# The tail of a mixture-of-experts kernel: TensorE forms the weighted sum of two expert rows, four gather buffers

## The chip, the cores and the metric

The kernel runs on one core of a Trainium2 chip. The metric is the time of one execution on the device in microseconds, as the median of the runs. A profiled execution has a time of its own, and its span runs from the first to the last instruction.

## The reference, cut to what matters

The program is a two-part transformer. What the change touches is the very end: the last mixture-of-experts layer, the residual, and the final norm. `second_block` ends so (`h` has 1024 tokens of 1024 features behind 16 meta tokens, which are cut off):

```
v = rms_norm_2(h, norm2_g[l])
h = h + hier_moe(v, ...)           # each token: 2 of 16 experts, weighted
return rms_norm_2(h[:, N_META:], final_g)

# in hier_moe
y = y + comb[:, e:e + 1] * (he @ exp_w2[e])     # comb: two weights per token, else 0
```

So for each token: h + w0 * (row of its first expert) + w1 * (row of its second expert), then an RMS norm over the features with a gain.

## The kernel before

`moe_phase` (line 2598) is the last of the phases. Tokens are sorted by expert into slots; 31 tiles of 128 slots (`NTILE`) are computed one after another. For each tile j, POOL fetches 128 normed token rows with an indirect DMA (`slots_in`, 2715) into one of two halves of `xs`, TensorE transposes them (`slots_t`, 3037), multiplies them with the expert's weights (`up`, 3045; `down`, 3057), ACT copies the result from PSUM (`YP`) to `yt` (2808), and POOL stores it to the DRAM tensor `expert_out` (2722). The weights pass through `stage`, five slots of 1024 columns: SP loads them, ACT rounds them to `whi`, DVE makes the rest `wlo` (`split_w`, 2837).

When all tiles are stored comes the tail, which is what the change rewrites. It goes over 8 token tiles (`NTT`) of 128 tokens, each 128 partitions by 1024 features in `ht`:

- POOL (2736 to 2747) waits for the last stores, and then for each token tile t issues two indirect DMAs of 512 KB, one for each of the token's two experts, into `yg[:, t % 3]`. There are three such buffers, so from t = 3 on it waits until tile t - 3 is added (`comb_done`).
- DVE (`combine`, 2975) waits for the two gathers, and adds w0 times the first and w1 times the second to `ht` by two instructions (2977, 2978). `cw` holds the weights, one for each partition and tile. The order on DVE is: combine(0), and then for each t: combine(t + 1), wait for the reciprocal root of tile t, multiply tile t by it and by the final gain (2987).
- ACT (2825 to 2831) waits for `comb_done` of tile t, squares it into `stage[:, 0]` with a running sum (2827), and turns the sum into the reciprocal root by Ln (2829) and Exp (2831). Each of the two needs its own load of a function table.
- SP (2708 to 2710) stores each finished tile to `y`.

TensorE has nothing to do in the tail. All engines work in the order in which their instructions are written; what passes between them are semaphores. `yg` lies in the space of the residual `E.X` that the tail no longer needs (columns 2 D to 8 D); `xs` lies behind it (8 D to 10 D). `TX` and `YP` are two PSUM tensors of 128x1024 f32.

Products on operands of the type `F32R` (experts, `whi`, `uhi`) and on plain `F32` both occur in the kernel. Plain f32 products with 512 columns are in the lines 1108 (sum of squares with a matrix of ones), 1130 and 3001 (router logits, two halves of 8 calls: 16 calls).

Of the kernel before, what the change touches and what calls it, by code (L numbers as in the profile page):

```python
# [19 lines left out]
ALU = mybir.AluOpType  # L20
# [3 lines left out]
P = 128  # L24
D = 1024
# [17 lines left out]
NTT = T // P  # L43
NSPARE = 15
NTILE = NE + NSPARE
# [90 lines left out]
def offsets(widths):  # L136
    at, n = {}, 0
    for name, w in widths:
        at[name] = (n, w)
        n += w  # L140
    return at, n


CONST_AT, CONST_N = offsets(CONST_WIDTHS)
# [4 lines left out]
def col(tile, at, name, j=None, w=1):  # L149
    o, width = at[name]  # L150
    if j is None:
        return tile[:, o:o + width]
    return tile[:, o + j:o + j + w]
# [14 lines left out]
def phase(nc, ctx):  # L168

    mine = []

    def sb(name, shape, dt=F32):
        return ctx.enter_context(nc.sbuf_tensor(f"{name}_{nc_tag(nc)}", shape, dt))

    def ps(name, shape, dt=F32):
        return ctx.enter_context(nc.psum_tensor(f"{name}_{nc_tag(nc)}", shape, dt))

    def sem(name):  # L180


        if not name.startswith("gp_"):
            mine.append(ctx.enter_context(nc.semaphore(f"{name}_{nc_tag(nc)}")))
            return mine[-1]
        return nc.alloc_semaphore(f"{name}_{nc_tag(nc)}")

    used = sorted(s.num for s in TAGS["used"])
    while used:
        n = 1  # L190
        while n < len(used) and used[n] == used[0] + n:
            n += 1
        nc.gpsimd.sem_clear(range(used[0], used[0] + n))
        used = used[n:]
    TAGS["used"] = mine
    return sb, ps, sem
# [5 lines left out]
def load_exp_ln(nc):  # L202

    nc.scalar.preload_act_table_set("natural_log_exp_and_others")
# [2393 lines left out]
def moe_phase(nc, E, dram):  # L2598


    with ExitStack() as ctx:
        sb, ps, sem = phase(nc, ctx)
        NS, R = 5, 8
        flat = E.X[:].rearrange("p k n -> p (k n)")
# [1 line left out]
        rows_of = [sb(f"token_rows{i}", [P, D])[:] for i in range(1)]  # L2606
        xs = flat[:, 8 * D:10 * D].rearrange("p (t n) -> p t n", n=D)
        yt = flat[:, 0:2 * D].rearrange("p (t n) -> p t n", n=D)
        yg = flat[:, 2 * D:8 * D].rearrange("p (t r n) -> p t r n", r=2, n=D)
        ht = sb("h_tokens", [P, NTT, D])  # L2610
        fgain = sb("final_rows", [P, D])
        rows_of += [fgain[:]]
        stage = sb("expert_stage", [P, NS, D])
# [20 lines left out]
        cw = sb("comb_w", [P, 2, NTT])  # L2634
# [3 lines left out]
        idx = sb("slot_index", [P, 2 * NTT], mybir.dt.uint32)  # L2638
        tcmp = flat[0:1, 2 * D + 2560:2 * D + 2560 + NSPARE * NE].rearrange("p (s e) -> p s e", e=NE)
        tsum, texp = sb("spare_count", [1, NSPARE]), sb("spare_expert", [1, NSPARE], mybir.dt.int32)  # L2640
        TX, YP = ps("slots_t", [P, D]), ps("expert_out", [P, D])
# [4 lines left out]
        wr_in, small_in, wr_ready, t_done, copied, squared, ms_ready, rs_ready, half_done, half_copied, logits_done = (  # L2646
            sem(n) for n in ("router_loaded", "small_loaded", "router_ready", "transposed", "copied", "squared",
                             "mean_square_ready", "rstd_ready", "logits_t_done", "logits_t_copied", "logits_done"))
# [5 lines left out]
        w_hi, w_lo, used = sem("expert_hi_ready"), sem("expert_lo_ready"), sem("expert_used")  # L2654
        u_hi, u_lo, h_t, silu_done, h_ready, h_hi, h_lo, y_ready = (sem(n) for n in (
            "slots_hi_ready", "slots_lo_ready", "hidden_t_done", "silu_done", "hidden_ready", "hidden_hi_ready",
            "hidden_lo_ready", "expert_out_ready"))
        idx_ready, fgain_in = sem("index_ready"), sem("final_gain_loaded")
        xs_in, y_out = [sem(f"gp_slots_loaded{i}") for i in range(2)], [sem(f"gp_expert_stored{i}") for i in range(2)]
        y_in = [sem(f"gp_expert_gathered{i}") for i in range(3)]  # L2660
        comb_done, f_sq, f_ms, f_rs, out_ready, steps = (sem(n) for n in (
            "combined", "final_squared", "final_mean", "final_rstd_ready", "out_ready", "dve_steps"))
        load_exp_ln(nc)
        block = ctx.enter_context(nc.Block())

        units, first_up, first_down = [], {}, {}
        for j in range(NTILE + 1):
# [6 lines left out]
        NU = len(units)  # L2674
        ahead = {}
        for j in range(NTILE + 1):
            end = first_up[j + 1] if j + 1 < NTILE else first_down[NTILE - 1] if j + 1 == NTILE else NU
            start = first_up[j] if j < NTILE else first_down[NTILE - 1]
# [34 lines left out]
        @block.gpsimd  # L2713
        def _(eng):
            def slots_in(j):
                if j >= 2:
                    eng.wait_ge(t_done, NTT + j - 1)
                eng.indirect_dma_start(
                    out=xs[:, j % 2, :], out_offset=None, in_=dram["normed"][:, :],
                    in_offset=bass.IndirectOffsetOnAxis(ap=inv[:, j:j + 1], axis=0)).then_inc(xs_in[j % 2], 16)  # L2720

            def expert_out(j):
                eng.wait_ge(y_ready, j + 1)
                eng.dma_start(dram["expert_out"][P * j:P * j + P, :], yt[:, j % 2, :]).then_inc(y_out[j % 2], 16)

            for s in range(NU_ROWS):
                eng.wait_ge(u_stored[s], 16 * ((NTT - s + NU_ROWS - 1) // NU_ROWS))
            eng.wait_ge(inverse_ready, 1)
            slots_in(0)
            slots_in(1)  # L2730
            for j in range(NTILE + 2):
                if j + 2 < NTILE:
                    slots_in(j + 2)
                if j >= 2:
                    expert_out(j - 2)
            for b in range(2):
                eng.wait_ge(y_out[b], 16 * ((NTILE - b + 1) // 2))
            eng.wait_ge(idx_ready, 1)
            for t in range(NTT):
                if t >= 3:  # L2740
                    eng.wait_ge(comb_done, t - 2)
                for r in range(2):
                    eng.indirect_dma_start(
                        out=yg[:, t % 3, r, :], out_offset=None, in_=dram["expert_out"][:, :],
                        in_offset=bass.IndirectOffsetOnAxis(ap=idx[:, NTT * r + t:NTT * r + t + 1], axis=0)).then_inc(y_in[t % 3], 16)
            for b in range(3):
                eng.wait_ge(y_in[b], 32 * ((NTT - b + 2) // 3))

        @block.scalar
        def _(eng):  # L2750
# [83 lines left out]
        def _(eng):  # L2834
            chain = Chain(eng, steps)
# [122 lines left out]
            for j in range(NTILE + 1):  # L2958
# [13 lines left out]
                for n in ahead[j][4:]:  # L2972
                    split_w(n)

            def combine(t):
                eng.wait_ge(y_in[t % 3], 32 * (t // 3 + 1))
                chain(eng.scalar_tensor_tensor(ht[:, t, :], yg[:, t % 3, 0, :], cw[:, 0, t:t + 1], ht[:, t, :], ALU.mult, ALU.add))
                eng.scalar_tensor_tensor(ht[:, t, :], yg[:, t % 3, 1, :], cw[:, 1, t:t + 1], ht[:, t, :],
                                         ALU.mult, ALU.add).then_inc(comb_done, 1)

            combine(0)
# [8 lines left out]
        def _(eng):  # L2990
            ident, ones = (col(E.con, CONST_AT, n) for n in ("ident", "ones"))
# [36 lines left out]
            for s in range(NTT):  # L3028
                mm = eng.matmul(POS[:, NE * s:NE * NTT], before_b[:] if s == 0 else ones_b[:], rows[:, 0:NE * (NTT - s)],
                                start=s == 0, stop=s == NTT - 1, skip_group_check=True)  # L3030
            mm.then_inc(pos_done, 1)
            eng.wait_ge(places_ready, 3)
            for i in range(2 * NTT):
                mm = eng.matmul(INV[:, 0:2 * NTILE], col_hot[:, i, :], tok_at[:, i, :], start=i == 0, stop=i == 2 * NTT - 1)
# [22 lines left out]
            def down(j, c):  # L3057
                n = first_down[j] + c
                eng.wait_ge(w_lo, n + 1)
                uh, ul = (u[:, j % 2, P * c:P * c + P] for u in (hhi, hlo))  # L3060
                for lhs, w, first, last in ((uh, whi, c == 0, False), (uh, wlo, False, False), (ul, whi, False, c == 1)):
                    for q in range(2):
                        mm = eng.matmul(YP[:, 512 * q:512 * q + 512], lhs, w[:, n % R, 512 * q:512 * q + 512],  # L3063
                                        start=first, stop=last)
                mm.then_inc(used, 1)

            slots_t(0)
            for j in range(NTILE + 1):
                if j < NTILE:
                    eng.wait_ge(u_lo, j + 1)  # L3070
                    if j >= 2:
                        eng.wait_ge(h_ready, j - 1)
                    for i in range(3):
                        up(j, i)
                if j >= 1:
                    eng.wait_ge(h_ready, j)
                    if j >= 2:
                        eng.wait_ge(h_lo, j - 1)
                    for c in range(2):
                        mm = eng.transpose(HT[:, P * c:P * c + P], hid[:, (j - 1) % 2, P * c:P * c + P], ident)  # L3080
                    mm.then_inc(h_t, 1)
                if j < NTILE:
                    up(j, 3)
                if j + 1 < NTILE:
                    slots_t(j + 1)
                if j >= 1:
                    eng.wait_ge(h_lo, j)
                    if j >= 2:
                        eng.wait_ge(y_ready, j - 1)
                    for c in range(2):  # L3090
                        down(j - 1, c)

# [295 lines left out]
```

## Time and profile before

| | us |
|---|---|
| median of 3 runs | 3211.17 |
| lowest, highest | 3204.91, 3211.19 |
| profiled execution | 3202.6 |
| its span | 3200.8 |
| tail: first gather issued to the end of the span | 3153.7 to 3200.8 |
| TensorE busy, whole span | 2804.8 (88%) |
| DVE, ACT busy, whole span | 1668.0 (52%), 1297.0 (41%) |

Times of rows are counted from the start of the span. TensorE is the busiest engine over the whole span, but it is idle in the tail, so the shares of the whole say nothing about the stage that is changed; that stage is read from its own rows. A record of a matmul has a modelled end: the distance between the starts of two that follow each other is the better measure of what one costs. The granted clock is given as a share of 2.4 GHz.

### The profile page before, as it was taken

The numbers are of one execution on the slowest core, as the hardware profiler recorded it, in microseconds if no ns is written. First come the engines' busy times: TensorE is split into PE (matmuls) and PEld (weight loads), VectorE is DVE, ScalarE is ACT, GpSimd is POOL, SyncE is SP. The second block draws the span as 40 slices with busy tenths as digits, with TensorE's granted clock in tenths as the row PEclk, the third lists the DMA queues.
The fourth block names the chain that finished last, engine by engine and source line by source line (L and its number), as shares of the span: only waits on it lengthen the run. The fifth ranks groups of instructions, "written<-read, shape, count | busy, mean of one in ns | idle before, by whom it ended". The sixth has DMA issues, their size and how long they took to land. (4 is left out here: it accounts for less than half of the span.)

```text
span 3200.8 us, 36024 instructions
## 1 busy us (share of the span) xinstructions
PE 2804.8 (88%) x13684; PEld 2195.9 (69%) x13684; DVE 1668.0 (52%) x2723; ACT 1297.0 (41%) x2204; POOL 196.3 (6%) x283
## 2 busy tenths in 40 slices
PE   7999998987887999995986999999989899588883
PEld 3777885656776868883654799987856588376672
DVE  5566545657774340013773356641134482688885
ACT  4444212446775141123442231111324411487886
POOL 0000000110000000000000000000000030011112
PEclk8999998989998999996998999999989999799997
DMA  5233444533303042222124123322353251599996
GB/s 230 97 132 119 171 148 122 153 100 97 80 20 120 7 152 76 89 79 87 33 83 157 61 83 103 129 96 79 112 169 80 58 180 33 198 346 346 366 357 236
DMA packets 143999, 431.05 MB, mean 135 GB/s; under 512 B 19874, under 2 KB 44194, under 8 KB 142548
## 3 DMA queue, kind: packets, MB, share of 16 engines
q1 hardware_dynamic: 99572, 264.52, 24.7%
q0 software_dynamic: 26512, 93.80, 8.5%
q10 hardware_dynamic: 17744, 70.43, 6.0%
q8 instruction: 109, 1.79, 0.2%
q14 instruction: 62, 0.51, 0.1%
HBM read 322.21 MB, written 106.47 MB: 134 GB/s over the span
## 5 line engine op out<-in xcount | busy, mean ns | idle before, releaser
L1099 PE MATMUL acc<-act_hi,w_hi 128*128 128x512 f32 (+3 forms) x2512 | 721.5, 376 | 62.4 <-DVE act_lo L856 41.5
L1099 PE MATMUL acc<-act_lo,w_hi 128*128 128x512 f32 (+3 forms) x2512 | 701.0, 368 | 0.0
L1099 PE MATMUL acc<-act_hi,w_lo 128*128 128x512 f32 (+3 forms) x2512 | 699.3, 367 | 0.0
L1099 PEld LDWEIGHTS acc<-act_hi,w_hi 128*128 128x128 f32 x2512 | 449.1, 189 | 165.3 <-DVE w_lo L761 57.6
L761 DVE TENSOR_TENSOR w_lo<-w_stage,w_hi 128x1024 fp32r<-128x1024 f32 x126 | 154.3, 1225 | 737.7 <-ACT w_hi L582 737.7
L1099 PEld LDWEIGHTS acc<-act_lo,w_hi 128*128 128x128 f32 x2512 | 447.0, 190 | 75.8
L1099 PEld LDWEIGHTS acc<-act_hi,w_lo 128*128 128x128 f32 x2512 | 446.1, 189 | 76.4
L582 ACT ACTIVATE w_hi<-w_stage 128x1024 fp32r<-128x1024 f32 x126 | 133.1, 1057 | 846.8 <-PE acc L1099 819.7
L2843 DVE SCALAR_TENSOR_TENSOR expert_lo<-expert_stage,params,expert_hi 128x512 fp32r<-128x512 f32 x248 | 172.5, 747 | 64.2 <-ACT expert_hi L2759 64.0
L1949 DVE TENSOR_REDUCE max<-scores 128x1 f32<-128x256 f32 (+6 forms) x256 | 117.4, 484 | 149.2 <-PE scores L2092 148.3
L2759 ACT ACTIVATE expert_hi<-expert_stage,params 128x512 fp32r<-128x512 f32 x248 | 163.2, 713 | 64.3 <-DMA expert_stage<-in_exp_w 30.4
L2132 PE MATMUL outputs<-probs_t,v_ones 128*128 128x512 f32 (+2 forms) x392 | 172.1, 520 | 1.9 <-ACT probs_t L1893 1.9
L1893 ACT ACTIVATE probs_t<-scores_t 128x512 f32<-128x512 f32 (+4 forms) x196 | 100.2, 513 | 119.9 <-PE scores_t L2118 116.9
L2110 PE MATMUL scores_t<-q_stack,k_hi 128*128 128x512 f32 (+4 forms) x196 | 122.6, 625 | 2.5 <-ACT q_rows L1917 2.5
L1480 DVE TENSOR_REDUCE stats<-scores 128x1 f32<-128x1280 f32 (+1 forms) x72 | 100.7, 1398 | 44.0 <-PE scores L1592 44.0
L3052 PE MATMUL expert_up<-expert_hi,slots_hi 128*128 128x512 f32 x248 | 101.7, 410 | 7.1 <-DVE slots_lo L2851 7.1
L693 ACT ACTIVATE out_stage<-acc 128x512 f32<-128x512 f32 (+1 forms) x162 | 78.0, 544 | 64.7 <-PE acc L1099 64.7
L1407 ACT ACTIVATE probs<-scores,stats 128x1280 f32<-128x1280 f32 (+1 forms) x80 | 92.1, 1153 | 25.8 <-DVE stats L1481 24.7
L2088 PE MATMUL scores<-k_hi,q_stack 128*128 128x256 f32 (+6 forms) x256 | 95.0, 374 | 5.5 <-DVE max L1949 2.6
L3054 PE MATMUL expert_up<-expert_hi,slots_lo 128*128 128x512 f32 x248 | 98.5, 397 | 0.0
L3053 PE MATMUL expert_up<-expert_lo,slots_hi 128*128 128x512 f32 x248 | 98.2, 396 | 0.0
L2092 PE MATMUL scores<-k_lo,q_rows 128*128 128x256 f32 (+6 forms) x256 | 92.2, 367 | 0.0
(409 smaller groups left out, 4210.8 us busy)
## 6 DMA issues: line engine op xcount, KB each, us to landing
expert_stage<-in_exp_w SPq DMA_DIRECT2D x186, 512.0 KB, 6.3
w_stage<-in_w_in SPq DMA_DIRECT2D x43, 512.0 KB, 4.2
rope<-out_stage ACTq DMA_DIRECT2D x26, 640.0 KB, 3.6
proj<-out_stage ACTq DMA_DIRECT2D x26, 640.0 KB, 5.0
slots_out<-residual POOLq DMA_DIRECT2D x31, 512.0 KB, 6.7
w_stage<-in_ab_w_in SPq DMA_DIRECT2D x26, 512.0 KB, 4.7
w_stage<-in_gla_w_in SPq DMA_DIRECT2D x25, 512.0 KB, 4.7
residual<-in_adaln_w POOLq DMA_DIRECT2D x24, 512.0 KB, 3.8
```

The source lines that it names most:

```text
L582: eng.activation(whi[:, w % 2, :], stage[:, w % NSTG, :], ACT.Copy).then_inc(w_hi, 1)
L761: eng.tensor_tensor(wlo[:, w % 2, :], stage[:, w % NSTG, :], whi[:, w % 2, :].bitcast(F32), ALU.subtract).then_inc(w_lo, 1)
L1099: mmi = eng.matmul(a[:, t, 0:n], lhs[:, j.w % 2, kb:kb + P], rhs[:, c0 + k, off:off + n], start=first, stop=last)
L1480: chain(eng.tensor_reduce(st[:, q % 4, 0, 0:u.rows], s, AX, ALU.max))
L1893: eng.activation(pT[0:w, q % 3, c0:512], ST[q % 2][0:w, c0:512], ACT.Exp, scale=SCALE).then_inc(exped, 1)
L1949: eng.tensor_reduce(mx[:, n % 2, h, pc:pc + 1], SP[p % 3][:, 0:k1 - k0], AX, ALU.max).then_inc(max_done, 1)
L2110: eng.matmul(s[:, c0:512], kh[:, c, tok:tok + P], qs[:, n % QS, c0:512], start=True, stop=False)
L2132: eng.matmul(O[n % 2][:, c0:512], v1[0:w, u.pair % VS, u.side, tok // P, :], pT[0:w, q % 3, c0:512], start=fox and b == 0, stop=b == len(u ...
L2759: ins = eng.activation(whi[:, n % R, c], stage[:, n % NS, c], ACT.Copy, scale=gain_of(2 * i + q))
L2843: ins = eng.scalar_tensor_tensor(wlo[:, n % R, c], stage[:, n % NS, c], gain_of(2 * i + q), whi[:, n % R, c].bitcast(F32), ALU.mult, ALU.s ...
L3052: eng.matmul(UP[j % 2][:], uh, wh, start=k == 0, stop=False)
L3054: mm = eng.matmul(UP[j % 2][:], ul, wh, start=False, stop=k == KD - 1)
```

## The change

Six of the eight token tiles (all but 0 and 4) are "mixed". For each of them DVE builds two diagonal matrices of 128x128, the identity times the token weights, in slots 1 and 2 of `stage`, behind its last weight split. TensorE then forms, for each half of 512 features, diag(w0) times the first gathered rows plus diag(w1) times the second, by two plain f32 products that accumulate in PSUM; the result goes alternately to `TX` and `YP`. DVE adds it to `ht` by one instruction in place of two. Tiles 0 and 4 keep the old two instructions. The gather buffers become four, the last of which lies where `xs` was; so POOL waits also for the last slot transposes.

```
-        yg = flat[:, 2 * D:8 * D].rearrange("p (t r n) -> p t r n", r=2, n=D)
+        NG = 4
+        yg = flat[:, 2 * D:10 * D].rearrange("p (t r n) -> p t r n", r=2, n=D)
...
+        mixed = [t for t in range(NTT) if t not in (0, 4)]
+        diag = stage[:, 1:3, :].rearrange("p a (b n) -> p (a b) n", n=P)
+        MIX = [TX, YP]
...
             eng.wait_ge(idx_ready, 1)
+            eng.wait_ge(t_done, NTT + NTILE)
             for t in range(NTT):
-                if t >= 3:
-                    eng.wait_ge(comb_done, t - 2)
+                if t >= NG:
+                    eng.wait_ge(comb_done, t - NG + 1)
...
+            eng.wait_ge(w_lo, NU)
+            for i, t in enumerate(mixed):
+                for r in range(2):
+                    eng.tensor_scalar(diag[:, 2 * i + r, :], col(E.con, CONST_AT, "ident"), cw[:, r, t:t + 1], None,
+                                      ALU.mult).then_inc(diag_ready, 1)
...
             def combine(t):
-                eng.wait_ge(y_in[t % 3], 32 * (t // 3 + 1))
+                if t in mixed:
+                    i = mixed.index(t)
+                    eng.wait_ge(mixed_ready, i + 1)
+                    eng.tensor_tensor(ht[:, t, :], MIX[i % 2][:], ht[:, t, :], ALU.add).then_inc(comb_done, 1)
+                    return
+                eng.wait_ge(y_in[t % NG], 32 * (t // NG + 1))
...
+            eng.wait_ge(diag_ready, 2 * len(mixed))
+            eng.wait_ge(y_ready, NTILE)
+            for i, t in enumerate(mixed):
+                eng.wait_ge(y_in[t % NG], 32 * (t // NG + 1))
+                if i >= 2:
+                    eng.wait_ge(comb_done, mixed[i - 2] + 1)
+                for q in range(2):
+                    for r in range(2):
+                        mm = eng.matmul(MIX[i % 2][:, 512 * q:512 * q + 512], diag[:, 2 * i + r, :],
+                                        yg[:, t % NG, r, 512 * q:512 * q + 512], start=r == 0, stop=r == 1)
+                mm.then_inc(mixed_ready, 1)
```

## Rows read from the trace of the kernel before

**Rows 1.** The chain that ended last, tail: start us, us, what.

```profile
3163.07 1.15 ACT expert_stage L2827 x2
3164.23 1.28 ACT L2829
...
3196.49 1.28 DVE h_tokens L2987
```

**Rows 2.** Groups by line, 3146.2 to 3201: busy us, mean ns, idle time before.

```profile
L2987 DVE SCALAR_TENSOR_TENSOR h_tokens<-h_tokens,final_rstd,final_rows 128x1024 f32<-128x1024 f32 x8 | 10.3, 1284 | 6.0 <-ACT final_rstd L2831 6.0
L2829 ACT ACT_TABLE_LOAD x8 | 10.3, 1283 | 0.1
L2827 ACT ACTIVATE expert_stage<-h_tokens 128x1024 f32<-128x1024 f32 x8 | 8.3, 1042 | 12.8 <-DVE h_tokens L2978 12.8
L2829 ACT ACTIVATE final_rstd<-final_sum_sq,eps 128x1 f32<-128x1 f32 x8 | 2.4, 295 | 0.1
L2831 ACT ACTIVATE final_rstd<-final_rstd 128x1 f32<-128x1 f32 x8 | 1.6, 203 | 0.1
L2827 ACT ACTIVATION_READ_ACCUMULATOR expert_stage<-h_tokens 128x1 f32 x8 | 1.5, 186 | 0.0
```

**Rows 3.** DVE and ACT in order of time: start us, us, instruction [idle before].

```profile
3160.43 1.28 DVE L2977 SCALAR_TENSOR_TENSOR h_tokens<-residual,comb_w,h_tokens 128x1024 f32<-128x1024 f32 x1 [14.30 <-DMA residual<-slots_out,slot_index]
3163.79 1.28 DVE L2977 SCALAR_TENSOR_TENSOR h_tokens<-residual,comb_w,h_tokens 128x1024 f32<-128x1024 f32 x1 [0.76 <-DMA residual<-slots_out,slot_index]
3167.24 1.04 ACT L2827 ACTIVATE expert_stage<-h_tokens 128x1024 f32<-128x1024 f32 x1
3171.53 1.28 DVE L2987 SCALAR_TENSOR_TENSOR h_tokens<-h_tokens,final_rstd,final_rows 128x1024 f32<-128x1024 f32 x1 [0.36 <-ACT final_rstd L2831]
...
3192.20 1.04 ACT L2827 ACTIVATE expert_stage<-h_tokens 128x1024 f32<-128x1024 f32 x1
```

**Rows 4.** Stretches: us, busy by engine (count), granted clock, DMA share, GB/s.

```profile
3149.20:3153.80 4.60, 0.00 (x0) 0.00 (x0) 0.00 (x0) 1.02 (x1) 0.62 (x2) 1.00 0.28 114
3154.00:3201.00 47.00, 0.00 (x0) 0.00 (x0) 30.30 (x24) 32.92 (x48) 15.84 (x16) 0.50 0.74 268
3161.30:3163.80 2.50, 0.00 (x0) 0.00 (x0) 1.71 (x3) 0.73 (x1) 0.50 (x1) 0.50 0.98 357
50.20:54.50 4.30, 4.30 (x6) 1.81 (x6) 0.84 (x2) 3.37 (x4) 0.00 (x0) 0.50 0.77 278
2797.98:2802.20 4.22, 4.22 (x10) 3.35 (x11) 0.00 (x0) 1.20 (x2) 0.00 (x0) 0.50 0.63 241
```

**Rows 5.** DVE's groups by line and shape in the expert phase.

```profile
L2851 DVE TENSOR_TENSOR slots_lo<-slots_t,slots_hi 128x1024 fp32r<-128x1024 f32 x31 | 37.7, 1217 | 2.5 <-ACT slots_hi L2766 2.5
L2923 DVE TENSOR_SCALAR slot_tmp<-expert_up 128x128 f32<-128x128 f32 x1 | 0.3, 292 | 0.0
```

**Rows 6.** POOL's gathers: the first with a wait, the slowest issue, landing times.

```profile
3163.30 0.94 POOL L2743 DMA_INDIRECT residual<-slots_out,slot_index  x1 [2.36 <-DVE h_tokens L2978]
3167.91 1.56 POOL L2743 DMA_INDIRECT residual<-slots_out,slot_index  x1 [0.30 <-issue]
DMA to landing us min/median/max: 4.1/6.2/7.7
```

**Rows 7.** Plain f32 products of lines 3001 and 1130: ns min/median/max, first and last start.

```profile
L3001 PE MATMUL expert_up<-residual,router_w x32: 592/592/607, 2729.3 to 2750.4; 128*20 128x512 f32 x32
L1130 PE MATMUL branch_acc<-branch_work,consts x8: 590/592/596, 2223.2 to 2226.2; 128*128 128x512 f32 x8
```

**Rows 8.** TensorE in order of time, products of line 1108 at granted clock 0.50.

```profile
50.19 1.19 PE L1108 MATMUL acc<-square_sums,consts 128*128 128x512 f32 x1 [1.71 <-PEq L229]
52.03 1.91 PE L1108 MATMUL acc<-square_sums,consts 128*128 128x512 f32 x2
52.88 1.06 PE L1108 MATMUL acc<-square_sums,consts 128*128 128x512 f32 x1
```

**Rows 9.** One more stretch, columns as in rows 4.

```profile
1502.00:1512.00 10.00, 10.00 (x18) 5.12 (x19) 2.29 (x5) 3.78 (x3) 0.00 (x0) 0.50 0.15 59
```

More of the change, by code:

```diff
@@ L2659, in moe_phase @@
         xs_in, y_out = [sem(f"gp_slots_loaded{i}") for i in range(2)], [sem(f"gp_expert_stored{i}") for i in range(2)]
-        y_in = [sem(f"gp_expert_gathered{i}") for i in range(3)]
+        y_in = [sem(f"gp_expert_gathered{i}") for i in range(NG)]
+        diag_ready, mixed_ready = sem("weight_diagonals_ready"), sem("outputs_mixed")
         comb_done, f_sq, f_ms, f_rs, out_ready, steps = (sem(n) for n in (
@@ L2738, in _ @@
             eng.wait_ge(idx_ready, 1)
+            eng.wait_ge(t_done, NTT + NTILE)
             for t in range(NTT):
-                if t >= 3:
-                    eng.wait_ge(comb_done, t - 2)
+                if t >= NG:
+                    eng.wait_ge(comb_done, t - NG + 1)
                 for r in range(2):
                     eng.indirect_dma_start(
[L2744 to L2747, printed above, removed]
+                        out=yg[:, t % NG, r, :], out_offset=None, in_=dram["expert_out"][:, :],
+                        in_offset=bass.IndirectOffsetOnAxis(ap=idx[:, NTT * r + t:NTT * r + t + 1], axis=0)).then_inc(y_in[t % NG], 16)
+            for b in range(NG):
+                eng.wait_ge(y_in[b], 32 * ((NTT - b + NG - 1) // NG))
         @block.scalar
@@ L2973, in _ @@
                     split_w(n)
-            def combine(t):
-                eng.wait_ge(y_in[t % 3], 32 * (t // 3 + 1))
-                chain(eng.scalar_tensor_tensor(ht[:, t, :], yg[:, t % 3, 0, :], cw[:, 0, t:t + 1], ht[:, t, :], ALU.mult, ALU.add))
-                eng.scalar_tensor_tensor(ht[:, t, :], yg[:, t % 3, 1, :], cw[:, 1, t:t + 1], ht[:, t, :],
+            eng.wait_ge(w_lo, NU)
[3 more added lines that the diff above has]
+                                      ALU.mult).then_inc(diag_ready, 1)
+            def combine(t):
+                if t in mixed:
[4 more added lines that the diff above has]
+                eng.wait_ge(y_in[t % NG], 32 * (t // NG + 1))
+                chain(eng.scalar_tensor_tensor(ht[:, t, :], yg[:, t % NG, 0, :], cw[:, 0, t:t + 1], ht[:, t, :], ALU.mult, ALU.add))
+                eng.scalar_tensor_tensor(ht[:, t, :], yg[:, t % NG, 1, :], cw[:, 1, t:t + 1], ht[:, t, :],
                                          ALU.mult, ALU.add).then_inc(comb_done, 1)
```

## The prediction

> **What bounds the kernel now.** The change touches only the last 55 us, so I read the chain of waits there first: it shows which engine sets the end. After the last expert output is stored and the first gather has landed, the chain is ACT alone: square, table load, Ln, table load, Exp, again and again until the last DVE multiplication [rows 1]. The grouped lines of the same stretch give the pieces [rows 2]. For a token tile ACT has 1.042 (square) + 0.186 (accumulator read) + 1.283 + 0.295 + 1.283 + 0.203 = 4.29 us, which overlap a little at the joints; the table loads are 2.57 of it. The order of time says what a tile really costs: the second square starts at 3167.24 and the eighth at 3192.20, which is six steps of 4.16 us [rows 3]. ACT waits for DVE once, 12.8 us before the first square [rows 2]; behind that it has no gap. DVE has three instructions of 1.28 us a tile, 3.9 us, and a rest of 0.36 us in which it waits for ACT's rstd (the idle time of L2987) [rows 2, 3]. So DVE is nearly full and yet not the bound. TensorE does nothing from 3149.2 on; its granted clock is 1.00 until 3153.8 and 0.50 from 3154 to the end, the lower of its two levels (1.2 GHz) [rows 4].
>
> **The change, part by part.**
>
> *DVE's additions in six tiles.* Two instructions (1.280 + 1.285 us) become one tensor_tensor of 128x1024 with one operand in PSUM. The nearest row is L2851, same shape, PSUM and SBUF operands: 1.217 us [rows 5]. That frees 1.35 us of DVE a tile. On the path it is worth nothing while ACT needs 4.16 us a tile: DVE only waits longer for the rstd. Bound: if DVE did set the pace it would be 6 x 1.35 = 8.1 us (a rival below).
>
> *Twelve diagonal matrices.* Each is a tensor_scalar of 128x128. The nearest row is L2923, 0.292 us (with a PSUM operand); so at most some 12 x 0.3 = 3.6 us, and not below 0; I take the row [rows 5]. They stand behind the last hidden_lo, which ends at 3146.1, so they are through by 3149.8. DVE idles from there until 3160.43 (14.3 us) [rows 3]. Nothing else queues behind them before the gather: cost 0. Without that cover it would be 3.6.
>
> *The new waits.* POOL waits for the last slot transposes, long done when the last expert is computed: 0 to 0.1 us. TensorE waits for diagonals and the last expert output, done by 3150.3: 0.
>
> *Four gather buffers.* The two gathers of tile 3 go out right behind the first six, some 2 us earlier, not behind the addition of tile 0 (3163.30) [rows 6]. Nothing waited for that tile: after tile 1 DVE has no idle time on a gather. So the gain is 0. The cost is bounded by the load on the engines: between 3161.3 and 3163.8 both tile 3 and tiles 1 and 2 would be in flight at a DMA share of 0.98 [rows 4]; if it took a third of those 2.5 us, tile 1 would land 0.8 us later. If the requests of one queue go in turn, 0. Tile 0 landed at 3160.43 and tile 1 by 3163.79, 3.4 us apart, although the six gathers of tiles 0 to 2 were issued back to back, before the one at 3163.30 [rows 3, 6]; that is how requests served in turn would land, and I take 0.
>
> The Trainium skill (DMA: Bandwidth & Descriptors, section on queues, rings and completion order) says that each DMA engine goes round between queue rows, but consumes one row's ring in ring order. By that rule the term is 0, by equal sharing 0.8; the landings above are on its side.
>
> *The matrix products: the term that counts.* Both operands are plain f32, not the rounded type of the experts. What does such a product cost? Line 3001 is called 16 times with 512 columns and shows 32 records, so a call is two records [rows 7]. Line 1130, same type, 128x128 weights and 512 columns: 8 records whose starts run from 2223.2 to 2226.2, so 0.427 us each at the full clock, 0.592 for the last to come out. At clock 0.50 the records of L1108 start at 50.19, one more, 52.03 and 52.88: 0.85 each, and 0.98 for the first (1.84 for the first two) [rows 8]. A mixed tile is 4 calls, 8 records: 8 x 0.427 = 3.4 us at the full clock, 6.8 us at the half one.
>
> Tile 1 is the first. It can't start before its gather lands (3163.79), and by then TensorE has been idle for 14 us and runs at 0.50. How long until the clock rises? After two other rests the clock stayed at 0.50 for 4.3 (50.2 to 54.5, f32 products) and 4.2 us (2798.0 to 2802.2) of continuous products, and was up behind that [rows 4]. I take 4.3: in it 0.98 + 3.9 x 0.853 is 4.9 records; the other 3.1 take 1.3 us; 0.17 for the last to come out: 5.8 us. So tile 1 is mixed at 3169.6, the DVE addition (1.22 and two handovers of about 0.04) ends at 3170.85, and ACT's second square starts at 3170.9 where it started at 3167.24: **+3.6 us**. Bounds of this term: TensorE at full clock throughout, 3.58 in place of 5.8: +1.4; at half clock for all eight, 0.98 + 6 x 0.853 + 1.06 = 7.2: +5.0. Below +1.4 it can't go, since 3.58 + 1.29 stands between the landing and the square.
>
> *What is late next.* With squares at 3170.9, 3175.1, 3179.2, 3183.4, 3187.5, 3191.7, 3195.9 for tiles 1 to 7, is each tile ready? Tile 2: TensorE 3169.4 to 3173.0; behind DVE's multiplication for tile 0 it is added at 3174.3. Tile 3: TensorE 3173.0 to 3176.4; DVE gets to it after tile 1's multiplication (rstd at 3175.1), done 3177.8. Tile 4, not mixed, as before: multiplication and two additions end 3183.1, 0.3 us ahead. Tile 5: its gather can only be issued when tile 1 is added (3170.9), two issues of 0.94 to 1.56 us and a landing of 6.2, at most 7.7 us put it at about 3179.3 (to 3181) [rows 6]; TensorE has rested some 3 us, is perhaps slow again, and ends at 3182.9 to 3186.6; DVE turns to it at 3186. It fits. Tiles 6 and 7 have 1 us or more to spare. The pace stays 4.16, the end moves by the 3.6 of tile 1. DVE's multiplication for tile 0 stands behind the addition of tile 1, so y's first store starts 3.5 us later. Of the stores only the last lies on the path, the 3 us from the end of the last L2987 (3196.49 + 1.28) to the end of the span [rows 1], and that stays.
>
> **Sum.** The profiled execution took 3202.6 us (span 3200.8); with +3.6 it is 3206.2. It lies 8.6 us below the median of the runs shown, 3211.17, so on the median: 3211.17 + 3.6 = **3214.8 us**.
>
> **The rivals.**
>
> A. *TensorE stays at the half clock through the tail.* Then a mixed tile takes 6.8 us against ACT's 4.16 and TensorE is the bound. Squares: tile 1 at 3172.2, tile 2 at 3172.2 + 6.8 = 3179.1, tile 3 at 3185.9, tile 4 at 3190.1 (not mixed, TensorE gains a step), tile 5 at 3194.2, tile 6 at 3199.6, tile 7 at 3206.4, against 3192.2: +14, 3225. For it: from 1502 to 1512 TensorE was busy for all 10 us, with products of other shapes than here, and the clock stayed at 0.50 [rows 9]. Against it: the products of 50.2 are of the very kind that is added, and both stretches above were back at full clock after 4.2 and 4.3 us, and tiles 1 to 3 run back to back for 12.6 us. It decides from the point where a tile on TensorE takes more than 4.16 us. Chance 0.10. The Trainium skill (TensorE: Matmul & The Clock Gate, section on a second failure mode) describes such small rests between groups bringing the clock down repeatedly; this would be that case, and no row of this tail can show it yet.
>
> B. *Tile 5 comes late.* Four buffers tie its gather to the addition of tile 1, which is now 4.4 us later than before (3166.4). Landing at 3181, a full half-clock burst of 7.2 us and the addition: 3189.5 against a square due at 3187.5, so +2.0 on top: 3216.8. With gathers of tiles slowed by stores up to 3218. Chance 0.12.
>
> C. *TensorE's clock is up for tile 1, or rises at once:* +1.4, 3212.6. Against it: the row of clock 0.50 over the whole tail. Chance 0.06.
>
> D. *DVE is the true pace (the other side).* It is nearly full, its rest of 0.36 us is small, and if ACT's gapless look hid a dependence on it, 8.1 us less 3.6 for tile 1 would come off: -4.5, 3206.7. Against it: DVE waits for ACT's rstd in all eight tiles, and ACT has no gap; the squares stand 0.1 us behind the Exp, not behind an addition. It would decide only if a square began at the end of an addition. Chance 0.07.
>
> **From cases to numbers.** Forecast 0.65. The three executions timed and the profiled one lie between 3202.6 and 3211.2, so a measurement tells about 0.2% (6.4 us) from no change; the forecast itself is within it. Slower by over 0.2%: A (0.10), half of B (0.06), and of the forecast 0.07, where its upper bounds (+5.0, +0.8) meet scatter: 0.23. Faster by over 0.2%: D with scatter, 0.06. The rest 0.71. The low end of the range is the sum against the profiled execution, 3206; the high end takes in B and the upper bounds, and leaves A out: 3220.
>
> **What would show it.** Right: records of the new product 0.85 us apart at first and 0.43 later, 48 in all; the second square at about 3170.9 by the old clock of the stage, with ACT idle some 3.6 us before it, released by the DVE addition; then 4.16 us a tile; L2977 and L2978 twice each; DVE's wait for the rstd up by about 1.35 us a tile. Wrong: squares further apart than 4.16 behind mixed tiles (A, or B if only before tile 5), a gap below 2 us (C), squares closer than 4.16 (D), a first gather that lands at another time than 7 us after the last store.

## The result and the profile after

| | us |
|---|---|
| before, median of 19 runs | 3207.33 |
| after, median of 19 runs | 3213.15 (3208.61 to 3216.45) |
| ratio of after to before | 1.0018, 95% interval 1.0010 to 1.0025 |
| profiled execution after, its span | 3211.45, 3209.7 |
| first gather issued to the end of the span, before | 3200.8 - 3153.7 = 47.1 |
| the same, after | 3209.7 - 3159.5 = 50.2 |

By the ratio the changed kernel is 0.18% slower. That is 5.8 us, of which the tail explains 3.1 in this profile. The first experiment, the unchanged kernel compared with itself, moved the ratio by 0.13%, so this ratio alone does not prove a slowdown; the tail, which repeats to 0.1 us in unchanged kernels (47.1 and 47.0), does. One execution of the kernel before, slower than the rest by half, is in its 19 runs and not in the ratio.

The groups of the tail of the changed kernel, 3151.8 to 3210 (columns as in rows 2):

```profile
L3119 PE MATMUL slots_t<-residual,expert_stage 128*128 128x512 f32 x24 | 12.7, 680 | 15.9 <-DMA residual<-slots_out,slot_index 15.9
L3005 DVE SCALAR_TENSOR_TENSOR h_tokens<-h_tokens,final_rstd,final_rows 128x1024 f32<-128x1024 f32 x8 | 10.3, 1283 | 11.1 <-ACT final_rstd L2838 11.1
L2836 ACT ACT_TABLE_LOAD x8 | 10.3, 1283 | 0.1
L2834 ACT ACTIVATE expert_stage<-h_tokens 128x1024 f32<-128x1024 f32 x8 | 8.4, 1044 | 15.8 <-DVE h_tokens L2996 12.7 <-DVE h_tokens L2992 3.1
L2992 DVE TENSOR_TENSOR h_tokens<-slots_t,h_tokens 128x1024 f32<-128x1024 f32 x3 | 3.7, 1222 | 6.1 <-PE slots_t L3119 6.1
```

ACT's table loads and squares cost what they cost before [rows 2]. The squares (L2834) have a second wait, which was not there before: 3.1 us for L2992, the new addition. DVE's wait for ACT's rstd has grown from 6.0 to 11.1 us, and DVE waits for TensorE's products too, 6.1 us of it for tile 1. What DVE was relieved of turned into waiting.

In order of time it is one place only. TensorE, DVE and ACT around tile 1 (columns as in rows 3):

```profile
3168.73 1.06 ACT L2834 ACTIVATE expert_stage<-h_tokens 128x1024 f32<-128x1024 f32 x1 [12.73 <-DVE h_tokens L2996]
3169.27 5.45 PE L3119 MATMUL slots_t<-residual,expert_stage 128*128 128x512 f32 x8 [14.33 <-DMA residual<-slots_out,slot_index]
3174.55 3.60 PE L3119 MATMUL expert_out<-residual,expert_stage 128*128 128x512 f32 x8
3174.82 1.22 DVE L2992 TENSOR_TENSOR h_tokens<-slots_t,h_tokens 128x1024 f32<-128x1024 f32 x1 [6.12 <-PE slots_t L3119]
3176.08 1.06 ACT L2834 ACTIVATE expert_stage<-h_tokens 128x1024 f32<-128x1024 f32 x1 [3.07 <-DVE h_tokens L2992]
3180.26 1.04 ACT L2834 ACTIVATE expert_stage<-h_tokens 128x1024 f32<-128x1024 f32 x1
...
3201.06 1.04 ACT L2834 ACTIVATE expert_stage<-h_tokens 128x1024 f32<-128x1024 f32 x1
```

The gather of tile 1 is there 9.8 us after the first issue (3169.27 - 3159.47; 10.1 before). TensorE works on it for 5.45 us, the addition takes 1.22, and the second square comes 7.35 us behind the first, not 4.17. From the third on they are 4.16 us apart again, up to the eighth.

The granted clock, in stretches (columns as in rows 4; the engines are PE, PEld, DVE, ACT, POOL):

```profile
3169.30:3172.80 3.50, 3.50 (x4) 1.45 (x5) 0.00 (x0) 3.44 (x5) 2.08 (x3) 0.50 1.02 408
3172.80:3181.50 8.70, 8.70 (x21) 3.63 (x19) 4.76 (x4) 5.55 (x10) 4.19 (x4) 1.00 0.70 254
```

Half clock (1.2 GHz) for some 3.6 us from the first product at 3169.27, then full clock (2.4 GHz) for the rest of tile 1 and for tiles 2 and 3.

### The profile page after: what moved, and what is told of

Read it like the earlier page. It is cut to its first block and busy times, and to the rows that moved or that the text cites. A ratio compares the mean times of both kernels' runs of the same rounds, so it can differ in the third digit from the quotient of the medians.

```text
span 3209.7 us, 36133 instructions
## 1 busy us (share of the span) xinstructions
PE 2831.3 (88%) x13732; PEld 2206.4 (69%) x13732; DVE 1661.6 (52%) x2729; ACT 1296.8 (40%) x2204; POOL 197.8 (6%) x283
```

## The experiments

The change's ratio says 5.8 us and its tail 3.1. Three theories: (1) ACT paces the tail with 4.16 us a tile, the mixing of the first mixed tile is the cost, and the rest is scatter of the long part ahead of the tail; (2) the rest is a real cost ahead of the tail; (3) DVE's share of the work counts, so that less work on DVE makes the tail shorter.

| kernel | expert tiles | tail | ratio, interval |
|---|---|---|---|
| before | 373.2 | 47.1 | |
| changed | 376.8 | 50.2 | 1.0018, 1.0010 to 1.0025 |
| same_again | 377.0 | 47.0 | 1.0013, 1.0004 to 1.0022 |
| changed_again | 371.2 | 51.6 | one execution |
| late_tiles | 377.2 | 47.0 | 1.0004, 0.9992 to 1.0017 |
| from_tile2 | 384.3 | 50.1 | one execution |
| kept_warm | 383.4 | 48.8 | one execution |
| one_addition | 377.4 | 45.8 | one execution |
| tables_before | 375.6 | 43.2 | 0.9989, 0.9978 to 1.0001 |
| tables_after | 367.1 | 45.9 | 1.0006, 0.9993 to 1.0019 |
| buffers_tables | 373.8 | 40.9 | 0.9986, 0.9973 to 0.9998 |
| late_tables | 370.2 | 44.8 | 0.9993, 0.9981 to 1.0005 |

Expert tiles: from the first slot transpose (L3042 in before) to the first gather's issue; tail: from there to the end of the span; us of the profiled execution of each. A ratio is to the kernel before, timed beside it; "one execution" means that there is no ratio.

**The kernel before, once more.** No edit.

> The kernel before, unchanged: how far do ratio and profile move with no edit at all? Tail (first gather issued to the end of the span) 47.1 us as before. Theory 1 (the change costs the 3.1 us of the tail and the other 2.5 us of its ratio are scatter of the long part ahead of it): ratio within 0.1% of 1, and the 31 expert tiles take another time than the 424 us of before by a microsecond or more. Theory 2 (the rest is a real cost ahead of the tail, brought by the larger program): ratio 1.000 and the same stages to a few tenths of a microsecond, so that the 4 us by which the expert tiles of the changed kernel are longer stand out.

Measured: tail 47.0; ratio 1.0013, an interval that leaves out 1. The same program, compared with itself, comes out 0.13% slower, so the interval of such a ratio is too narrow to be taken at its word. Its expert tiles took 377.0 us, as the changed kernel's did. The expectation under theory 1 asked for a ratio within 0.1%; it was missed by a little, and on the side of more scatter. Theory 2 has lost its evidence; that there is no cost at all ahead of the tail isn't shown.

**The changed kernel, once more.** No edit to it.

> The changed kernel once more, a second look at the same instructions. Theory 1: tail 50.2 us again, give or take the moment at which TensorE's clock rises in tile 1 (3.4 us after its first product in the first look; 4.3 would add 0.45 us); expert tiles anywhere between 367 and 377 us, as the looks so far show. Theory 2 (a cost ahead of the tail): expert tiles again 376.8 us.

Measured: tail 51.6, where 50.2 was expected, or 50.65 with a clock that rises at 4.3 us. Tile 1 and tile 5 in order of time:

```profile
3168.37 6.43 PE L3119 MATMUL slots_t<-residual,expert_stage 128*128 128x512 f32 x8 [14.68 <-DMA residual<-slots_out,slot_index]
3174.64 3.60 PE L3119 MATMUL expert_out<-residual,expert_stage 128*128 128x512 f32 x8
3178.07 3.60 PE L3119 MATMUL slots_t<-residual,expert_stage 128*128 128x512 f32 x8
3184.17 5.38 PE L3119 MATMUL expert_out<-residual,expert_stage 128*128 128x512 f32 x8 [2.50 <-DMA residual<-slots_out,slot_index]
3189.39 3.60 PE L3119 MATMUL slots_t<-residual,expert_stage 128*128 128x512 f32 x8
```

and its stretches:

```profile
3168.40:3173.90 5.50, 5.50 (x7) 2.40 (x8) 0.00 (x0) 3.20 (x6) 1.88 (x2) 0.50 1.03 419
3184.20:3188.00 3.80, 3.80 (x5) 1.67 (x6) 3.33 (x3) 3.74 (x7) 0.94 (x1) 0.55 1.01 395
```

The clock rose some 5.6 us after the first product, not 3.6, so tile 1 took 6.43 us and ACT waited 4.51 us. Its landing was 10.15 us after the first issue, 0.35 later. The change costs 3.1 us in one execution and 4.5 in the other, depending on when the clock rises. After a rest of 2.5 us the clock was at 0.50 once more, and tile 5 took 5.38 us; the squares stayed 4.16 apart, since there ACT is behind. The expert tiles took 371.2 us with the very program that took 376.8: 5.6 us of difference with no edit.

**Only tiles 5, 6 and 7 mixed.**

```
-        mixed = [t for t in range(NTT) if t not in (0, 4)]
+        mixed = [5, 6, 7]
```

> The changed kernel with tiles 5, 6 and 7 mixed only. Theory 1 (ACT paces the tail; mixing costs only where the first mixed tile has no slack against ACT's 4.16 us a tile): tile 5's gather lands some 5 us before ACT is due for it, so even a start at half clock (5.5 us and the addition of 1.3) fits: ACT has no gap, tail 47.1 us, ratio 1.000. Theory 2 (a cost ahead of the tail): tail 47.1, ratio 1.0008 as with the change. Theory 3 (DVE's share counts): less than 47.1 by up to 4 us.

Measured: tail 47.0, squares 4.15 to 4.17 apart, ACT's only wait the one ahead of the first square. Four buffers, six of the twelve matrices, three mixings and three cheaper additions together changed nothing. It was close, though: TensorE took 5.51 us for tile 5, and its addition (3192.21, 1.22 us) ended 0.5 us before the square it had to be ready for (3193.91). With the 6.43 us that changed_again needed for its tile 1 it would have been late by some 0.4 us, by an estimate from these rows. The ratio, 1.0004, does not tell theory 1 from theory 2.

**Tile 1 left to DVE.**

```
-        mixed = [t for t in range(NTT) if t not in (0, 4)]
+        mixed = [2, 3, 5, 6, 7]
```

> The changed kernel with tiles 2, 3, 5, 6 and 7 mixed, tile 1 by DVE alone. Theory 1: the cost does not go away with tile 1 but passes to tile 2, since gathers land 3.4 us apart and ACT asks every 4.16: tile 2 lands 13.2 us after the first issue, 5.5 us of mixing from half clock and 1.3 us of addition make 20.0 against a due time of 17.7; so the third square waits some 2.3 us, tail 49.4 us. A rival that lays the cost on tile 1 alone: 47.1.

TensorE's first mixing in order of time:

```profile
3178.36 6.66 PE L3119 MATMUL slots_t<-residual,expert_stage 128*128 128x512 f32 x8 [17.20 <-DMA residual<-slots_out,slot_index]
```

and ACT's second and third square:

```profile
3179.03 1.04 ACT L2834 ACTIVATE expert_stage<-h_tokens 128x1024 f32<-128x1024 f32 x1
3186.31 1.06 ACT L2834 ACTIVATE expert_stage<-h_tokens 128x1024 f32<-128x1024 f32 x1 [3.03 <-DVE h_tokens L2992]
```

The cost is not tile 1's own; it went over to tile 2. The wait was 3.0 us where 2.3 were expected: the mixing took 6.66 us where 5.5 had been assumed, and the gather landed at 12.7 us instead of 13.2, which took back 0.5 of that. Tail 50.1; the rival's 47.1 is out.

**TensorE kept busy until tile 1.** 16 products whose results are not used.

```
+            for _ in range(16):
+                eng.matmul(UP[0][:], diag[:, 0, :], diag[:, 0:4, :].rearrange("p b n -> p (b n)"), start=True, stop=True)
             for i, t in enumerate(mixed):
```

> The changed kernel with 16 f32 products on TensorE between the last expert tile and tile 1, whose results are not used, so that the clock does not fall. Theory 1: tile 1 takes 3.6 us on TensorE in place of 5.45, the second square waits 1.2 us in place of 3.1, tail 48.3 us. Theory 3: no statement. If it is not the clock but the landing of the gather that makes tile 1 late, the tail stays at 50.2.

TensorE's tile 1 in order of time:

```profile
3181.63 3.70 PE L3121 MATMUL slots_t<-residual,expert_stage 128*128 128x512 f32 x8 [1.47 <-DMA residual<-slots_out,slot_index]
```

ACT's second square:

```profile
3186.70 1.06 ACT L2834 ACTIVATE expert_stage<-h_tokens 128x1024 f32<-128x1024 f32 x1 [1.33 <-DVE h_tokens L2992]
```

and two stretches, the added products and the first three mixed tiles:

```profile
3166.20:3180.00 13.80, 13.80 (x32) 5.95 (x32) 1.51 (x2) 0.00 (x0) 7.18 (x8) 1.00 0.52 180
3181.60:3192.00 10.40, 10.37 (x24) 4.48 (x24) 4.64 (x4) 8.95 (x14) 6.20 (x7) 1.00 0.92 348
```

With the clock at 1.00 through tiles 1 to 3, tile 1 takes 3.70 us and ACT waits 1.33 (1.2 expected). Tail 48.8 (48.3 expected; the first square itself came 0.3 us later than in the changed kernel). So of the wait of 3.07 or 4.51 us in the changed kernel, 1.3 us is for putting f32 products into the path at all, and 1.7 to 3.2 for the half clock.

**One addition left out in every tile.** The first expert's row is left out of the output.

```
-                chain(eng.scalar_tensor_tensor(ht[:, t, :], yg[:, t % 3, 0, :], cw[:, 0, t:t + 1], ht[:, t, :], ALU.mult, ALU.add))
```

> The kernel before with the first of DVE's two additions left out in all eight tiles (the first expert's row is left out of the output): the most that relieving DVE could bring, with nothing added elsewhere. Theory 1 (ACT paces): squares stay 4.16 us apart; only tile 0 is ready 1.3 us sooner, tail 45.8 us. Theory 3 (DVE paces): squares come closer, up to 1.28 us a tile, tail down to 37.

Measured: 45.8, the expected figure; squares 4.16 to 4.18 apart. The waits of DVE in its tail (who waits, for whom: us in total, times, longest):

```profile
DVE h_tokens L2977 <- DMA residual<-slots_out,slot_index: 16.6, 2, 14.3
DVE h_tokens L2986 <- ACT final_rstd L2831: 13.7, 8, 2.9
```

DVE had 10.2 us less to do (L2977 of the kernel before [rows 3] eight times over) and the tail became 1.3 us shorter, by the first tile alone. DVE's wait for ACT went from 6.0 to 13.7 us. Theory 3 is refuted.

**ACT relieved: one table set for both functions.** Added ahead of ACT's last loop, to the kernel before and to the changed one:

```
+            eng.preload_act_table_set("natural_log_exp_and_others")
             for t in range(NTT):
                 eng.wait_ge(comb_done, t + 1)
```

> The kernel before with one edit: ACT loads the table set that has both Ln and Exp once, ahead of its last loop, so that the 16 loads of 1.28 us in the tail should fall to one, hidden in ACT's wait. Theory 1 (ACT paces): ACT needs 1.75 us a tile, DVE with 3.9 us becomes the bound; squares 3.9 us apart, the last tile's chain shorter by 2.6 us; tail 47.1 - 5 = 42 us, ratio 0.9985. Theory 3 (DVE paces already): squares stay 4.16 apart, only the 2.6 us of the last tile come off, tail 44.5.

> The changed kernel with the same edit: both engines relieved. Theory 1: now the gathers and TensorE set the order. Tile 1 is still added late (5.5 us of mixing), tiles 5 to 7 wait for gathers that are issued on the additions of tiles 1 to 3 and land some 5 us apart; squares of the last tile about 10 us sooner than in the changed kernel is not to be had; tail about 45 us, 5 us less than the changed kernel, yet 3 more than the kernel before with the same edit. Theory 3 (DVE's share is what was missing): it is faster than the kernel before with the edit by up to 8 us.

DVE's waits in the tail of the kernel before with this edit:

```profile
DVE h_tokens L2978 <- DMA residual<-slots_out,slot_index: 16.9, 4, 14.1
DVE h_tokens L2988 <- ACT final_rstd L2832: 0.6, 1, 0.6
```

The table loads are gone from the loop: Ln and Exp do not each need a load of their own, as "The kernel before" had it, once the set that has both is loaded ahead of it. DVE's wait for ACT fell from 6.0 to 0.6 us. Now DVE paces, with 3.71 us a tile (3.9 was expected, three records of 1.28 us and a little; the records overlap, as those of ACT do), but for two tiles at 4.7 and 4.9 us that waited for gathers. Tail 43.2 (42 expected: those two waits were missed). The changed kernel with the same edit: 45.9 (45 expected), 4.3 us less than the changed kernel, 2.8 more than the kernel before with it. Even with ACT out of the way the mixing loses, by the same first tile: its second square comes 6.73 us behind the first, where it is 3.39 without mixing.

**The same with four buffers, unmixed and mixed late.**

> The kernel before with four gather buffers and with the table set of Ln and Exp loaded once, no mixing. With the tables alone the tail was 43.2 us, and two of its steps were 4.7 and 4.9 us where DVE waited for gathers, the others 3.7. Theory 1 (the bound is now DVE with 3.7 us a tile, if gathers are issued one tile sooner): all steps 3.7, tail 41 us, ratio 0.998. A rival (the gathers are held by the transfer rate, not by the buffers): tail 43 as with the tables alone.

Measured: seven steps, 3.26 and six of 3.71 or 3.72; tail 40.9, ratio 0.9986. ACT's squares, two of eight:

```profile
3174.61 1.06 ACT L2830 ACTIVATE expert_stage<-h_tokens 128x1024 f32<-128x1024 f32 x1 [2.00 <-DVE h_tokens L2981]
3178.32 1.06 ACT L2830 ACTIVATE expert_stage<-h_tokens 128x1024 f32<-128x1024 f32 x1 [2.00 <-DVE h_tokens L2981]
```

ACT now waits 2.0 us a tile for DVE. The two waits for gathers had been the buffers', not the transfer rate's. This is the best tail: 6.2 us less than before, 9.3 less than changed. By the ratio it is 0.14% faster than before, but a comparison that moves by 0.13% with no edit cannot prove that. The tail can: 6.2 us stand against 0.1 us between the two profiles of the kernel before.

> The changed kernel with tiles 5, 6 and 7 mixed only, and the table set loaded once: mixing where TensorE has time, and ACT no longer the bound, so that DVE's relief of 1.35 us a tile can show. Theory 1: DVE needs 2.5 us for each of the last three tiles, but their gathers land some 4 to 5 us apart beside the stores of y, so steps fall from 3.7 to 3.5 at best and may rise to 4.5; tail 40 to 42 us, no better than the unmixed kernel with the same two edits by more than 1 us. A rival (the change was right and only misplaced): 38 us or less.

TensorE's tiles 5, 6 and 7 in order of time:

```profile
3176.53 6.58 PE L3120 MATMUL slots_t<-residual,expert_stage 128*128 128x512 f32 x8 [28.54 <-DMA residual<-slots_out,slot_index]
3182.94 3.60 PE L3120 MATMUL expert_out<-residual,expert_stage 128*128 128x512 f32 x8
3186.37 3.60 PE L3120 MATMUL slots_t<-residual,expert_stage 128*128 128x512 f32 x8
```

and ACT's squares of tiles 5 and 6:

```profile
3184.40 1.06 ACT L2835 ACTIVATE expert_stage<-h_tokens 128x1024 f32<-128x1024 f32 x1 [6.54 <-DVE h_tokens L2993]
3187.83 1.06 ACT L2835 ACTIVATE expert_stage<-h_tokens 128x1024 f32<-128x1024 f32 x1 [1.72 <-DVE h_tokens L2993]
```

Tail 44.8, where 40 to 42 was expected, and so 3.9 us worse than the same kernel unmixed. Tile 5's time had been laid on its gather, but the gather was there in time: TensorE started on it at 3176.53, and DVE was busy until 3177.3 with what stands before tile 5. What came late was the mixing, 6.58 us with most of it at half clock, and one step of 8.26 us instead of 3.71. Of these 4.55 us the half clock explains 3.0 (6.58 against 3.60); the other 1.6 is by an estimate from the same rows what mixing costs there even at full clock: TensorE starts only when the gather is there, and ACT no longer leaves slack. No run tested that by itself. The two steps behind it are 3.43 us, the time of TensorE's eight records, against DVE's 3.71 without mixing: at full clock and with ACT relieved, mixing gains 0.28 us a tile once it is under way.

## Why the prediction was right, point by point

**What bounds.** Right. ACT had no gap but the new one, and the pace stayed 4.16 us. DVE's rest before the multiplications of the late mixed tiles went from 0.36 to 1.74 us, as the forecast of about 1.35 more has it. That DVE's relief is worth nothing was shown by leaving an addition out altogether (one_addition), that ACT is the pace by relieving it (tables_before).

**The size of the path term.** Forecast +3.6 us with bounds +1.4 and +5.0; the two profiles gave +3.1 and +4.5, and at full clock the wait was 1.3 us. The terms: landing of tile 1 at 10.08 us behind the first issue, measured 9.8 and 10.15; records 0.427 and 0.853, 48 of them, as said; the addition 1.22, as said. What varied was the rise of the clock, taken as 4.3 us: 3.6 in the one, 5.6 in the other, and 2.8 to 6.0 over all kernels here (below). The two stretches it was taken from were too few to tell that spread; that the forecast lies between the two measured values is right in kind and partly luck in size.

**Twelve matrices.** Sized at 3.6 us, they took 2.43 and lay under DVE's idle time, as predicted. In order of time, changed kernel:

```profile
3151.81 2.43 DVE L2985 TENSOR_SCALAR expert_stage<-consts,comb_w 128x128 f32<-128x128 f32 x12
```

**Four buffers.** The extra gathers in flight did not delay tile 1 beyond 0.1 us; equal sharing was bounded at 0.8 in the forecast. That is how requests of one queue served in turn would land. The rule of the Trainium skill that was weighed (DMA: Bandwidth & Descriptors, queues, rings and completion order) agrees with these landings, and no run here tells more of it.

**Tile 5 (rival B).** Half of the premise came true in changed_again: the clock was down again after the rest of 2.5 us. But the landing at 3184.17 is 26.0 us after the first issue, where B has 27.3, and the mixing took 5.38 us, not 7.2. It stayed hidden, because ACT was late by then too. Rival B's extra 2 us did not appear in either profile. Rival A did not occur in the changed kernel: the clock rose within tile 1, each time. C is what kept_warm made by hand.

**The sum.** 3214.8 was forecast on the median then shown; 3213.15 was measured beside a median of 3207.33 for before. That the two figures lie 1.7 us apart is partly luck: the median that the forecast started from was 3.8 us too high, and the change it added 2.2 too low. From 3207.33 the same term gives 3210.9. The difference is 5.8 us against 3.6 forecast. 3.1 to 4.5 of it are in the tail; the remaining 1.3 to 2.7 us aren't found in any stage that repeats, and are less than the 0.13% (4.2 us) by which the unchanged kernel differed from itself. The expert tiles ahead vary from 367.1 to 384.3 us between profiles of programs whose expert tiles are the same. In the lowest of them the stretch reads (columns as in rows 4):

```profile
2781.90:3148.90 367.00, 308.02 (x1426) 247.06 (x1426) 292.03 (x399) 289.88 (x420) 61.28 (x60) 0.97 0.91 340
```

for tables_after, and for from_tile2:

```profile
2781.40:3165.60 384.20, 318.88 (x1426) 256.06 (x1426) 291.44 (x398) 288.01 (x419) 55.79 (x60) 0.93 0.89 325
```

The same 1426 records of products stand at a clock of 0.97 or 0.93, and took TensorE 308.0 or 318.9 us. The lower 325 GB/s says nothing by itself: 340 over 367.0 us and 325 over 384.2 us are the same bytes. Whether the half-clock stretches made the stage long or a longer stage, with more rests, brought the clock down, is open.

## What to carry to other kernels

Before work is moved off an engine, ask who waits for whom in the loop: here DVE was busy 91% of a step (3.77 of 4.16 us) and still not the bound; ACT was, with 2.6 us of table loads in every tile. After a rest of over 14 us TensorE began at half clock in all six profiles in which a mixed tile followed such a rest (5.07 to 6.66 us for a tile that takes 3.6 at full clock); a product put on a path after such a rest must be priced at that clock, and at the tile with the least slack. When the expected effect is 0.1% of a run, compare the kernel with itself first, and judge by the stage.

## What the runs showed that was not expected

- The moment at which TensorE's clock rises after a rest is not the same in two executions of one program: 3.6 us and 5.6 us after the first product, which made 5.45 or 6.43 us of one tile. Over all kernels it lies between 2.8 us (tables_after, a first mixed tile of 5.07 us) and 6.0 us (from_tile2, 6.66 us; late_tables 5.8 and 6.58 us). The stretches at half clock of tables_after and late_tables, from just behind the first product:

```profile
3158.70:3161.50 2.80, 2.80 (x4) 1.25 (x5) 0.00 (x0) 1.33 (x4) 2.19 (x3) 0.50 1.00 367
3176.60:3182.30 5.70, 5.70 (x7) 2.42 (x8) 0.70 (x1) 1.19 (x4) 0.00 (x0) 0.50 1.00 410
```

- A rest of 2.5 us, between tile 3 and tile 5, was enough for the clock to fall in changed_again, and so was one of 2.3 us in from_tile2 and of 2.46 us in kept_warm (5.40 us for tile 5 in both); in the changed kernel's first profile a rest of 2.2 us in the same place was not (granted clock 1.00 from 3181.6 to 3200).
- One table set serves Ln and Exp: loading it ahead of the loop took all 16 loads out of the loop.
- The expert tiles vary by 17 us between profiles, more than any two tails here differ (40.9 to 51.6 us).
